# Expert rows taken one by one instead of in pairs, with a changed plan, and the merge's gates by tanh instead of sigmoid

## What is computed

```python
def merge(pool_o, gla_o, mla_o, gz, branch_w, w_out):
    gates = sigmoid(gz).reshape(shp + (N_BRANCH, D_MODEL))
    m = (gates[..., 0, :] * (pool_o @ branch_w[0]) + gates[..., 1, :] * (gla_o @ branch_w[1])
         + gates[..., 2, :] * (mla_o @ branch_w[2]))
    return m @ w_out
...
x_lat = x_lat + g1 * y            # y = merge(...), g1 from the modulation of the layer
...
# peer, for each token and each of 8 heads, 16 experts chosen by their keys
g = softmax(top)
a = gelu(einsum('nd,nhjd->nhj', xs, u[eid]), approximate=False)
return einsum('nhj,nhjd->nd', g * a, v[eid])
```

## Time and profile before

| | us |
|---|---|
| median of 3 runs | 3435.36 (3432.03 to 3439.66) |
| the profiled execution | 3441.62 |
| its span, from first to last instruction | 3439.5 |
| PE busy | 2810.3 (82%) |
| PEld busy | 1750.6 (51%) |
| DVE busy | 1919.4 (56%) |
| ACT busy | 1111.6 (32%) |
| POOL busy | 853.5 (25%) |
| moved by DMA | 1071.76 MB, mean 312 GB/s |

### The profile page before, as it was taken

One profiled execution on the slowest core, in us unless ns is written; L12 is line 12 of the kernel. 1 busy time (PEld: TensorE's weight loads), 2 busy tenths in 40 slices (PEclk: granted clock), 3 DMA queues, 4 the chain that ended last, 5 costly groups with the idle time before them and its releaser, 6 DMA issues.

```text
span 3439.5 us, 40717 instructions
## 1 busy us (share of the span) xinstructions
PE 2810.3 (82%) x15162; PEld 1750.6 (51%) x15162; DVE 1919.4 (56%) x4582; ACT 1111.6 (32%) x3213; POOL 853.5 (25%) x772
## 2 busy tenths in 40 slices
PE   8999998989888999888775555699999986655555
PEld 6777887655545666564431111278788841211111
DVE  4564764566676556456676766422300256666665
ACT  2232002343574455323533232232310123323222
POOL 0000001234332333223344444200000034444443
PEclk9999999999999999999898776899999987776776
DMA  8264764989998999879999999733144299999998
GB/s 327 99 208 148 289 239 169 369 339 373 373 358 329 417 421 420 336 299 371 404 372 420 415 412 412 308 111 110 57 152 151 73 376 414 411 419 403 411 415 335
DMA packets 151780, 1071.76 MB, mean 312 GB/s; under 512 B 16668, under 2 KB 19356, under 8 KB 23200
## 3 DMA queue, kind: packets, MB, share of 16 engines
q0 software_dynamic: 110592, 805.36, 57.8%
q1 hardware_dynamic: 40992, 263.82, 20.5%
HBM read 1068.06 MB, written 1.05 MB: 311 GB/s over the span
## 4 chain that ended last, share of the span: by engine, by line
PE 51%; DMA 26%; DVE 12%; ACT 6%; issue 3%; POOL 2%; SPq 0%; DVEq 0%; POOLq 0%; ACTq 0%
PE bank L438 38%; DMA ring<-in_experts,eid 25%; PE bank L452 11%; DVE ring L1494 5%; POOL ring L1968 2%; ACT topk_work L1007 1%; ACT topk_work L1000 1%; DMA ring<-in_quads 1%; ACT topk_work L997 1%; ACT L997 1%; DVE state L1729 1%; PE bank L465 1%; PE bank L687 0%; DVE topk_work L1464 0%; PE bank L568 0%
## 5 line engine op out<-in xcount | busy, mean ns | idle before, releaser
L1968 POOL DMA_INDIRECT ring<-in_experts,eid x768 | 853.3, 1111 | 2563.2 <-PE bank L452 1284.2
L452 PE MATMUL bank<-ring,topk_work 64*64 64x512 f32 x6144 | 975.0, 763 | 557.6 <-ACT topk_work L1007 544.3
L1494 DVE CUSTOM_DVE_ANT_0 ring<-ring,h2tok 128x1024 f32<-128x1024 f32 x768 | 937.4, 1225 | 589.1 <-DMA ring<-in_experts,eid 574.9
L452 PEld LDWEIGHTS bank<-ring,topk_work 64*64 64x64 f32 x6144 | 234.7, 158 | 1185.5 <-ACT topk_work L1007 878.3
L997 ACT ACTIVATE topk_work<-topk_work 128x2 f32<-128x2 f32 x384 | 78.0, 203 | 1139.9 <-DVE topk_work L1494 1132.6
L438 PE MATMUL bank<-h_even,weights 128*128 128x256 f32 (+1 forms) x1280 | 293.2, 388 | 4.4 <-ACT h_even L1080 4.0
L438 PEld LDWEIGHTS bank<-h_even,weights 128*128 128x128 f32 (+1 forms) x1280 | 240.9, 190 | 60.8 <-issue 22.8
L438 PE MATMUL bank<-h_odd,weights 128*128 128x256 f32 (+1 forms) x1008 | 228.3, 382 | 0.0
L1007 ACT ACTIVATE topk_work<-const,topk_work 128x64 f32<-128x64 f32 x768 | 225.6, 341 | 0.2 <-ACT topk_work L1000 0.2
L438 PEld LDWEIGHTS bank<-h_odd,weights 128*128 128x128 f32 (+1 forms) x1008 | 187.5, 189 | 49.9 <-issue 23.8
L1000 ACT ACTIVATE topk_work<-topk_work 128x1 f32<-128x1 f32 x768 | 184.6, 287 | 12.6
(11 more groups left out here) (252 smaller groups left out, 3243.6 us busy)
## 6 DMA issues: line engine op xcount, KB each, us to landing
weights<-in_quads SPq DMA_DIRECT2D x151, 1024.0 KB
ring<-in_quads SPq DMA_DIRECT2D x84, 1024.0 KB, 4.9
ring<-in_experts,eid POOLq DMA_INDIRECT x768
weights<-in_quads SPq DMA_DIRECT2D x6, 768.0 KB
ring<-in_quads SPq DMA_DIRECT2D x6, 768.0 KB, 4.5
weights<-in_quads SPq DMA_DIRECT2D x12, 256.0 KB
xT<-in_xT SPq DMA_DIRECT2D x2, 1024.0 KB, 11.7
out<-state SPq DMA_DIRECT2D x4, 256.0 KB, 5.3
```

The source lines that it names most:

```text
L452: x = nc.tensor.matmul(acc[g][out, :], diag[mine, J % 4, :], ring[mine, J % RING, D + h * 512:D + (h + 1) * 512], start=first, stop=J % TI ...
L1494: v.tensor_tensor_reduce(row, row, h2tok[:, u // UNITS % 2, :], 1.0, 0.0, ALU.mult, ALU.add, dots[:, u % 2, j:j + 1]).then_inc(S["dot_done ...
L1968: pool.indirect_dma_start(ring[:, J % RING, :], None, d["experts"], bass.IndirectOffsetOnAxis(eid[:, u % 2, j:j + 1], 0)).then_inc(gathere ...
```

## The change

Three edits.

1. Rows are taken one by one on PE, ACT and DVE. A row's Gelu no longer waits for the second dot of a pair; there are 768 Gelus of one column for 384 of two. Row counts stand in place of pair counts; the places at which tile ends, softmax exponentials (`j == 5` for `j == 4`) and the last stage's turns are worked in stay where they were to within a row.
2. The plan: `LAG` is 4.0 for 5.0, a row's landing is its own, and in `breathe` the allowance of half a hole is fixed at entry and no longer moves with the clock.
3. The merge's gate is tanh(x/2) on ACT; DVE adds 1 and multiplies in one instruction; the factor 1/2 is put on G1 of the modulation by a small DVE instruction for each half of G1 and layer (4 in all), and the residual waits for it.

```diff
-PER_LOAD, LANDS, LAG = 2.5, 2.0, 5.0
+PER_LOAD, LANDS, LAG = 2.5, 2.0, 4.0
...
-            def emit(n):
-                landing = plan.row(2 * n + 1)
-                placed_now[n] = (len(job_log), landing)
-                plan.now = max(plan.now, landing + LAG) + 0.2
-                row_pair(n)
...
+            def emit(J):
+                landing = plan.row(J)
+                placed_now[J] = (len(job_log), landing)
+                plan.now = max(plan.now, landing + LAG) + 0.1
+                row(J)
...
-                for J in (2 * n, 2 * n + 1):
-                    plan.now += 0.95
-                    if (J + RING) // GROUP_ROWS == J // GROUP_ROWS:
-                        plan.gather()
-                cur["next"] = n + 1
+                plan.now += 0.95
+                if (J + RING) // GROUP_ROWS == J // GROUP_ROWS:
+                    plan.gather()
+                cur["next"] = J + 1
...
-                end = plan.now + hole
-                while cur["next"] < cur["limit"] and plan.row(2 * cur["next"] + 1) + LAG <= plan.now + hole / 2:
+                end, early = plan.now + hole, plan.now + hole / 2
+                while cur["next"] < cur["limit"] and plan.row(cur["next"]) + LAG <= max(plan.now, early):
...
-                m = n % 4 * 2
-
-                act.wait_ge(S["dot_done"], J + 2)
-                nc.scalar.activation(gel[:, m:m + 2], dots[:, par, j:j + 2], ACT.Gelu).then_inc(S["act_gelu"], 1)
-                act.wait_ge(S["act_gelu"], 3 * n + 1)
-                for c in range(2):
-                    nc.scalar.activation(gelw[:, m + c:m + c + 1], gel[:, m + c:m + c + 1], ACT.Copy,
-                                         scale=wts[:, par, j + c:j + c + 1]).then_inc(S["act_gelu"], 1)
+                m = J % 8
+
+                act.wait_ge(S["dot_done"], J + 1)
+                nc.scalar.activation(gel[:, m:m + 1], dots[:, par, j:j + 1], ACT.Gelu).then_inc(S["act_gelu"], 1)
+                act.wait_ge(S["act_gelu"], 2 * J + 1)
+                nc.scalar.activation(gelw[:, m:m + 1], gel[:, m:m + 1], ACT.Copy, scale=wts[:, par, j:j + 1]).then_inc(
+                    S["act_gelu"], 1)
                 if J >= 4:
 
-                    act.wait_ge(S["row_used"], J - 2)
-                for c in range(2):
-                    act.wait_ge(S["act_gelu"], 3 * n + 2 + c)
-                    nc.scalar.activation(diag[:, (J + c) % 4, :], ident_blk, ACT.Copy,
-                                         scale=gelw[:, m + c:m + c + 1]).then_inc(S["diag_ready"], 1)
+                    act.wait_ge(S["row_used"], J - 3)
+                act.wait_ge(S["act_gelu"], 2 * J + 2)
+                nc.scalar.activation(diag[:, J % 4, :], ident_blk, ACT.Copy, scale=gelw[:, m:m + 1]).then_inc(S["diag_ready"], 1)
...
-                    if placed[n][0] > now and not (placed[n][1] + DIAG_LAG <= when and reached(n, now, 2)):
+                    if placed[n][0] > now and not (placed[n][1] + DIAG_LAG <= when and reached(n, now, 4)):
...
-                            nc.scalar.activation(gate_buf(n)[:, m % 8, :], b[:, 0:TS], ACT.Sigmoid).then_inc(
+                            nc.scalar.activation(gate_buf(n)[:, m % 8, :], b[:, 0:TS], ACT.Tanh, scale=0.5).then_inc(
...
-                if n % TILE_PAIRS == 0 and n // TILE_PAIRS in (1, 2, 3):
-                    tile_out(n // TILE_PAIRS - 1)
+                if J % TILE_ROWS == 1 and J // TILE_ROWS in (1, 2, 3):
+                    tile_out(J // TILE_ROWS - 1)
...
-                    deep = 2 if n % TILE_PAIRS == 3 else 3
+                    deep = {1: 2, 7: 4}.get(n % TILE_ROWS, 6)
...
+                if q // 2 == G1:
+
+                    dve.wait_ge(*at("evicted", "mod", n, q))
+                    v.tensor_scalar(mods[:, n, q * 4:q * 4 + 4, :], mods[:, n, q * 4:q * 4 + 4, :], 0.5, None,
+                                    ALU.mult).then_inc(*mark("dve_step", ("halved", n, q)))
...
-                                v.tensor_tensor(tt, gate, b[:, 0:TS], ALU.mult).then_inc(
+                                v.scalar_tensor_tensor(out=tt, in0=gate, scalar=1.0, in1=b[:, 0:TS], op0=ALU.add,
+                                                       op1=ALU.mult).then_inc(
...
+                    if c % 4 == 0:
+                        dve.wait_ge(*at("halved", i, 2 * G1 + c // 4))
```

More of the change, by code:

```diff
@@ L438, in mm, with row @@
                 return nc.tensor.matmul(out, lhsT, rhs, start=first, stop=last, **kw)
-            def row_pair(n):
-                for J in (2 * n, 2 * n + 1):
-                    k, first = J // TILE_ROWS, J % TILE_ROWS == 0
-                    if first and J:
-                        for g in range(2):
-                            pe.wait_ge(*at("evicted", "acc", k - 1, g))
-                    pe.wait_ge(S["diag_ready"], J + 1)
-                    for h in range(2):
-                        out = slice(h * BLK, (h + 1) * BLK)
-                        for g in range(2):
-                            mine = slice(g * BLK, (g + 1) * BLK)
-                            x = nc.tensor.matmul(acc[g][out, :], diag[mine, J % 4, :],
-                                                 ring[mine, J % RING, D + h * 512:D + (h + 1) * 512],
-                                                 start=first, stop=J % TILE_ROWS == TILE_ROWS - 1, skip_group_check=True)
-                    x.then_inc(S["row_used"], 1)
+            def row(J):
+                k, first = J // TILE_ROWS, J % TILE_ROWS == 0
+                if first and J:
+                    for g in range(2):
+                        pe.wait_ge(*at("evicted", "acc", k - 1, g))
+                pe.wait_ge(S["diag_ready"], J + 1)
+                for h in range(2):
+                    out = slice(h * BLK, (h + 1) * BLK)
+                    for g in range(2):
+                        mine = slice(g * BLK, (g + 1) * BLK)
+                        x = nc.tensor.matmul(acc[g][out, :], diag[mine, J % 4, :],
+                                             ring[mine, J % RING, D + h * 512:D + (h + 1) * 512],
+                                             start=first, stop=J % TILE_ROWS == TILE_ROWS - 1, skip_group_check=True)
+                x.then_inc(S["row_used"], 1)
             def tile_sum(k):
@@ L948, in _ @@
                     cur["pace"] = 0.0
-                    rows_until(first_pair(p.beside + 1))
+                    rows_until(first_row(p.beside + 1))
                     tile_sum(2 * p.beside + 1)
@@ L1037, in rows_until @@
                     cur["next"] += 1
-                    row_pair(cur["next"] - 1)
+                    row(cur["next"] - 1)
             def rows_before(*key):
@@ new lines, in row @@
+            def row(J):
+                u, j = divmod(J, PTOP)
+                if j == 0:
+                    for m in range(2):
+                        if u % UNITS == 0:
+                            dve.wait_ge(*at("evicted", "ht", u // UNITS // 2, u // UNITS % 2, m))
+                dve.wait_ge(gathered[J % RING], 16 * (J // RING + 1))
+                row = ring[:, J % RING, 0:D]
+                v.tensor_tensor_reduce(row, row, h2tok[:, u // UNITS % 2, :], 1.0, 0.0, ALU.mult, ALU.add,
+                                       dots[:, u % 2, j:j + 1]).then_inc(S["dot_done"], 1)
+                if u + 1 < GROUPS * 2 * UNITS and (u + 1) not in LEADS:
+                    if j < PTOP // 2:
+                        choose(u + 1, 2 * j)
+                        choose(u + 1, 2 * j + 1)
+                if J % TILE_ROWS == 1 and J // TILE_ROWS in (1, 2, 3):
+                    tile_out(J // TILE_ROWS - 1)
+                if J % TILE_ROWS == 7 and J // TILE_ROWS in (1, 2, 3):
+                    add_tile(J // TILE_ROWS - 1)
+                if J == 5 * TILE_ROWS + 1:
```

67 lines of the change are left out of this document (22 added, 45 removed).

## The result

| | before | after |
|---|---|---|
| median, us (4 runs each) | 3437.51 (3432.03 to 3443.59) | 3489.06 (3481.90 to 3493.89) |
| ratio, 95% interval | | 1.0148 [1.0122, 1.0173] |
| profiled span, us | 3439.5 | 3487.8 |

The change makes the kernel 1.5% slower. The forecast was 3391 in a range of 3350 to 3434.

What follows compares the result with a forecast made beforehand. PE with holes was taken to bound 575 to 1790, queues the rows-only stages, both the merge. 23 + 13 + 5 + 5 + 2 + 3 - 4 - 3 = 44 us off 3441.6, 3397.6; less 6.2 to the median, 3391; range 3350 to 3434.

Steps and rivals of the forecast that it cites:

- What bounds the kernel: PE with its holes from 575 to 1790, PE and queues both in the merge, the queues in the rows-only stages.
- The term of LAG: Pass 1 and start of group 1: LAG 4.0 for 5.0 lengthens PE's waits, costing 15 and 8.5 us.
- the slack of 1.7 us: PE's rows: planned time left after the chain, 1.7 us for 2.6 with pairs; each wait can be 0.85 us longer.
- The term of the filled waits: 575 to 1500 and 1500 to 1790: the first row's matmuls fill PE's waits, gaining 38 and 22 us.
- The term of the switches: PE between weight-stationary groups and rows: up to 174 more switches at 0 to 0.1 us each, costing 3 us.
- the same 82 us: 575 to 1500: PE's holes, the most to be had there; the rule of `breathe` got no sum of its own.
- the forecast 5 of the queues and 2 of the end: Rows-only 2800 to 3400: more rows in flight gain 5 us; at the end the last row alone gains 2.
- Tanh's term of 3: Merge of pass 1: table loads of gates and Gelus go, credited with 3 us.
- my 18: Group 1: 13 us net from 1500 to 1790 and 5 us from the rows-only stage 1790 to 2215.
- The first, that the rows are bound by the queues anyway: Sooner slots wait in the queue, PE's holes stay in its stages; 9 us off, 3426; chance 0.18.
- The third, that tanh saves no loads: Merge: the 24 gates go on alternating with Gelus, so table loads stay; 3397; chance 0.11.
- The second rival: Pass 1 and start of group 1: PE waits twice for single rows, once for a pair; 3470; chance 0.13.

Runs made afterwards that it cites:

- the run without them: The kernel after with tanh in place of the rows' Gelu, so that exponential and row share a table: profiled span 3429.7 us for 3487.8.
- the six: Single rows with LAG 4.0, 5.0, 6.0, 7.0, 8.0 and 10.0: medians 3489.06, 3439.26, 3429.39, 3417.13, 3410.49 and 3436.01 us.
- LAG 5.0 with the faster plan: The kernel after with LAG 5.0 and 2.0 added to the plan's clock at each attention step: 3463.46 us, ratio 1.0070.

## Why the prediction was wrong

The step that failed is the price of the lower LAG, 23.5 us in the sum and 50 us measured. Two terms beside it were mis-sized too, the filled waits and the switches of PE.

**What bounds the kernel** stood. The merge is full in both (243 us), and the loss and the gains came in the stages that were named.

**The term of LAG failed**, on two steps. I set it at 15 + 8.5 = 23.5 us; it measured 50 in medians and 61 in spans. The first step was the slack of 1.7 us, taken as the time by which "each wait that occurs" grows. But it also decides which rows wait at all. ACT's own delays are 1.28 for a swap, 2.57 for two, and some more for an exponential that waits for DVE (1.72 in the timeline): by this count 2.6 of slack covers two swaps, 1.7 covers one. Both numbers were in the rows of before; I didn't lay them side by side. That the missing slack meets the swaps is shown by the run without them, which takes back 58 us with the order unchanged; that the limit lies at two swaps is not, as single rows with 2.7 of slack still lose 24 us to them and gain on up to LAG 8.0. The second was "a neighbour wait shrinks by it; I count half". In the attention it is the other way: PE's waits are 33.4 us for 14.4 and ACT's for PE 38.2 for 5.6, and the timeline shows one leading to the other.

**The term of the filled waits failed as well.** I took 1.1 us off each of 35 and 20 waits. With LAG left at 5.0, where the term of LAG is out, the waits of 575 to 1500 fell from 73.5 to 61.4, 12 us for the forecast 38, and from the first gather of group 0 to that of group 1 it still took 10 us more (925.6 for 916.0). In the mixer (402.6 for 395.4) other matmuls ate the gain: PE's busy time outside rows is 256.9 us for 248.3. In the attention (108.5 for 96.2) the waits for diagonals did not fall but rose, from the 14.4 above to:

```profile
PE bank L449 <- ACT topk_work L1000: 22.9, 8, 5.8
```

So the attention is where a single row fills no wait, and single rows at the old LAG gained nothing.

**The term of the switches failed too.** I gave 3 us, from 0 to 0.1 us a switch; the working behind it (8 times 0.235 twice) doubles the 1.88 of the earlier trace rows, which is for all 16 matmuls and holds the switch already. The starts of PE's matmuls in the merge have the price, with the same medians before, after, at LAG 5.0 and at LAG 8.0. Undisturbed it is 216 ns between two matmuls of a job and 429 between two groups of four of a row. Around a change it is 309 from a job to the row, 480 from the row's first group to its second, 539 from its last group to the job, and 320 from the job's first matmul to its second. That is 93 + 51 + 110 + 104 = 358 ns too much for each time that rows are taken between jobs, 0.18 us for a change. From the first gather of group 0 to the end of group 1 the changes are 401 after for 299 before, so some 18 us for my 3. In the mixer the other matmuls take 9 to 13 us more with single rows (LAG 4.0, 5.0 and 8.0), where pairs at LAG 4.0 take 2 more; with 124 to 132 changes for 92 the switches are 6 to 7 of it, and the rest stays open.

**The rule of `breathe`** did not belong into the same 82 us. It is worth 209 us to single rows; the forecast was safe there only because it was part of the change.

**What held.** Group 2 to the end gained 13.1 us for the forecast 5 of the queues and 2 of the end, the right way and nearly twice the size; the 600 us from 2862 carry 416 GB/s as the mean of their slices of 15 us, for 409 in the earlier trace rows and the 412 to 415 of my test:

```profile
GB/s 309 418 422 421 422 420 421 420 423 421 420 423 419 419 423 421 419 421 415 423 360 392 416 427 422 421 421 419 422 423 418 422 423 420 419 425 418 418 422 421
```

A row's matmuls start some 2.3 us after its own dot (dot at 3093.14, its weights at 3095.43). Tanh's term of 3 lies between the 4 and the nothing that were measured, neither of which can be told from zero. Gelu's table loads fell from 100 to 84 (forecast about 75), the gates' from 26 to none. Group 1 gained 11.6 for my 18 in the fast execution of LAG 5.0, and lost it again at 4.0. PE's busy time over 575 to 1500 did not rise above 843 but fell to 827. A small misreading: the stages without rows carry 57 to 327 GB/s in the earlier trace rows, not 73 to 327.

**The rivals.** The first, that the rows are bound by the queues anyway, had its sign at 409 GB/s, and 416 was measured. The third, that tanh saves no loads, is refuted: 49 loads fell to 4. The page that spoke for it, the Trainium skill, ScalarE: Activation LUTs, section Table sets: the hidden batching unit, does not list tanh with Gelu; the trace has no load between them, and between tanh and exponential none either, so there the page and the measurement agree on the second and differ on the first. The second rival, slower by slack at the rows that come 4.0 after their landing, had the sign, the cause and my threshold of 125 us of waits over 575 to 1790 (93.9, and from 1500 the 37.0 of the line below), and its 3470 was still 19 too low. Its picture was wrong in one thing: waits did not double, they were 43 for 35, each 2.2 us. The rest goes with ACT's waits, the lower clock and the switches; no run parts them. I gave it 0.13 on the ground that the long waits were those for a partner; the wait in rows 6 was, but one wait isn't the 35.

```profile
PE bank L449 <- ACT topk_work L1000: 37.0, 16, 8.6
```

**Still open**: 5 us at the start of pass 3, where the clock is 0.62 for 0.93 in 25 us with no rows about. Before it both have a rows-only stage, of 0.79 and 0.82. No experiment set out to change this.

## What to carry to other kernels

When a plan sets a distance between a transfer's landing and its use, hold it against the delays that the engines between really have, a table swap and whatever waits ahead of it in their order. Here 4.0 us was too short: a miss held up both in-order streams, and they went on waiting for each other. So when a grain is halved, go through every constant of the plan again from the trace (here 8.0 gave the lowest time of the six, and 4.0 was the wrong way), look at each loop that is fed by its own clock for the step at which it runs away, and count the changes between kinds of work and price them from start to start. Move one such constant alone before you put a result down to the structure: single rows are 1.1% faster or 1.5% slower than the pairs at 5.0 by this number, and the pairs would have to be tuned too for a fair match.

## What the runs showed of the hardware

- A table load takes 1.28 us and the function behind it starts at once (1019.54 + 1.28, 1020.84). Tanh shares a table with Gelu and one with the exponential: in the merge and in the attention no load stands between them.
- On PE, taking rows (64x64 weights, 64x512) between jobs (128x128 weights, 128x256) costs 0.36 us there and back at the granted clock of 1.00, in the merge, with the same medians in four kernels.
- The mean granted clock of the attention was mostly lower where PE stood still more: 1.00, 0.91, 0.93, 0.89 and 0.79 at 14, 14, 18, 25 and 35 us idle (LAG 8.0, before, pairs at LAG 4.0, LAG 5.0, after). Idle time alone doesn't set it, as 14 us went with 1.00 and 0.91, and 42 us of 150 with 0.82 (LAG 5.0 with the faster plan). PE's busy time grew as the clock fell, from 82 to 97 us between before and after, some 15 of the 36 us by which this stretch became longer, and a sum of waits misses them.
